# Expert stages of a two-layer diffusion block: the chain up to the first gather reordered, and the query passes of later heads planned further apart

## The reference

```python
def peer(h, w_q, sub_keys, u_tab, v_tab):           # 8 heads, 128 x 128 experts, top 16 per head
    q = (h @ w_q).reshape(b, L, PEER_HEADS, 2, D_HALF)
    scores = jnp.einsum("blhtd,htkd->blhtk", q, sub_keys)
    sv, si = lax.top_k(scores, PEER_TOPK)
    cand_s = sv[..., 0, :, None] + sv[..., 1, None, :]       # 256 candidates
    top_s, pos = lax.top_k(cand_s, PEER_TOPK)
    idx = jnp.take_along_axis(cand_i, pos, axis=-1)
    gate = softmax(top_s)
    act = gelu(jnp.einsum("tkd,td->tk", u_tab[idx], h))
    return jnp.einsum("tk,tkd->td", gate * act, v_tab[idx])

x = layer_norm(alpha * x + gate_row * sublayer((1 + scale) * x + shift))   # shift, scale, gate from c
```

## Time and profile before

| | us |
|---|---|
| median of 3 runs | 5075.4 (5074.77 to 5085.62) |
| profiled execution | 5070.65 |
| its span | 5068.9 |
| PE busy | 3558.4 (70%) |
| DVE busy | 3230.2 (64%) |
| POOL busy | 2215.4 (44%) |
| ACT busy | 1506.1 (30%) |
| first to last gather issued, context | 461.2 to 1210.6 |
| the same, latents of layer 0 | 1676.9 to 3038.9 |
| the same, latents of layer 1 | 3711.5 to 5042.1 |

### The profile page before, as it was taken

The page is one execution under the profiler, slowest core; times in us unless marked ns, Lnnn a source line. Parts: engine busy times, 40 slices in busy tenths (PEclk is TensorE's granted clock), DMA queues, the critical chain, the costliest instruction groups (busy, mean ns, idle before and its releaser), DMA issues. The chain is left out here.

```text
span 5068.9 us, 49208 instructions
## 1 busy us (share of the span) xinstructions
PE 3558.4 (70%) x15992; PEld 1832.1 (36%) x15992; DVE 3230.2 (64%) x6604; ACT 1506.1 (30%) x3708; POOL 2215.4 (44%) x1683
## 2 busy tenths in 40 slices
PE   7887888886678986555555557979888555555555
PEld 5576434332267443111111115877743111111111
DVE  5354687664464567776767766466456777777775
ACT  2342344343151224222222223243222222222221
POOL 3253444442032344555555552334324555555554
PEclk8888999998788998777777778899998777777777
DMA  5435999998602799999999992102268999999998
GB/s 182 171 121 198 390 413 407 415 424 362 231 22 101 274 359 393 416 411 418 403 423 417 411 424 81 67 1 92 84 270 350 415 419 411 417 414 417 420 414 375
DMA packets 251729, 1575.63 MB, mean 311 GB/s; under 512 B 42560, under 2 KB 49216, under 8 KB 65472
## 3 DMA queue, kind: packets, MB, share of 16 engines
q0 software_dynamic: 184320, 1342.26, 64.1%
q1 hardware_dynamic: 67152, 230.23, 12.3%
HBM read 1554.88 MB, written 17.50 MB: 310 GB/s over the span
## 5 line engine op out<-in xcount | busy, mean ns | idle before, releaser
L2337 PE MATMUL banks<-arena 128*64 128x512 f32 x5120 | 1621.0, 771 | 1136.3 <-ACT arena L2169 1135.6
L1953 POOL DMA_INDIRECT arena<-in_experts,arena x1280 | 1499.1, 1171 | 1681.4 <-PE banks L2337 1429.4
L2041 DVE CUSTOM_DVE_ANT_0 arena<-arena,token_copies 128x1024 f32<-128x1024 f32 x1280 | 1640.4, 1298 | 687.5 <-DMA arena<-in_experts,arena 631.5
L2337 PEld LDWEIGHTS banks<-arena 128*64 128x64 f32 x5120 | 391.5, 169 | 2218.4 <-ACT arena L2169 1569.5
L2162 ACT ACTIVATE arena<-arena 128x2 f32<-128x2 f32 x640 | 131.2, 205 | 1830.2 <-DVE arena L2041 1829.2
L281 POOL TENSOR_TENSOR wide_low<-wide_blocks,wide_high 128x1024 fp32r<-128x1024 f32 x136 | 343.5, 2548 | 552.2 <-ACT wide_high L271 552.2
L2169 ACT ACTIVATE arena<-arena 128x64 f32<-128x64 f32 x1280 | 376.0, 340 | 294.1 <-POOL arena L1820 252.7
L2218 PE MATMUL banks<-arena,wide_blocks 128*128 128x512 f32 (+3 forms) x960 | 315.2, 477 | 32.6 <-ACT arena L2071 23.7
L319 PE MATMUL banks<-activation_a,wide_high 128*128 128x512 f32 (+1 forms) x768 | 278.5, 363 | 8.5 <-ACT arena L343 2.7
L2289 PE MATMUL banks<-arena,wide_blocks 128*128 128x512 f32 x576 | 276.6, 618 | 0.0
L321 PE MATMUL banks<-activation_a,wide_low 128*128 128x512 f32 (+1 forms) x768 | 269.4, 351 | 0.0
(11 more groups left out here) (251 smaller groups left out, 4928.2 us busy)
## 6 DMA issues: line engine op xcount, KB each, us to landing
wide_blocks<-in_wide SPq DMA_DIRECT2D x168, 1024.0 KB, 4.8
arena<-in_experts,arena POOLq DMA_INDIRECT x1280, 10.8
pre_scan<-arena SPq DMA_DIRECT2D x16, 256.0 KB, 7.3
arena<-pre_scan SPq DMA_DIRECT2D x16, 256.0 KB, 5.2
residual<-in_tokens SPq DMA_DIRECT2D x6, 512.0 KB, 7.7
arena<-mod_rows SPq DMA_DIRECT2D x6, 512.0 KB, 6.8
norm_rows<-in_keys SPq DMA_DIRECT2D x3, 1024.0 KB, 6.0
pre_z<-arena SPq DMA_DIRECT2D x8, 256.0 KB, 7.4
```

The costliest lines, as they stand in the source:

```text
L1953: pool.indirect_dma_start(out=v.ring[:, g % RING], out_offset=None, in_=io["experts"], in_offset=bass.IndirectOffsetOnAxis(ap=c.idx[:, u % ...
L2041: last = nc.vector.tensor_tensor_reduce(out=u_row, in0=u_row, in1=k.copies[:, n % NJ], scale=1.0, scalar=0.0, op0=ALU.mult, op1=ALU.add, a ...
L2337: mm = nc.tensor.matmul(k.ps[j * QUAD:(j + 1) * QUAD, a + half], v.lhs[:, g % 4, j], v.ring[:, (g * NJ + j) % RING, D + half * BANK:D + (h ...
```

## The change

The stages that end the mixing get a new order of output products and four PSUM banks; the columns are loaded and completed there, into a tensor of their own (`k.nextmod`). In `stage_peer` the first two scores follow the second pass, the later scores stand inside the next pass or behind their own, the first masks stand behind the third gather, and the planned times of the passes are changed: `PROJ` becomes 17.5 for both NT (13 and 17 before), and with NT = 4 the passes from the thirteenth on are planned 16 units apart in place of 8. `stage_finish` is changed as `stage_merge` is.

```diff
-ARENA = A_ROWS + PC_N + HR_N + KT * 32 + 16 + 4 * 288 + 480 - 184
+ARENA = A_ROWS + PC_N + HR_N + KT * 32 + 16 + 4 * 288 + 480 - 200
...
+    k.nextmod = sb("peer_modulation", [P, 2, KT])
...
+def output_order(NT):
+
+    early = [(q, t) for q in range(2) for t in range(NT)]
+    late = [(2, 0), (2, 1), (3, 0)] + [x for t in range(2, NT) for x in ((2, t), (3, t - 1))] + [(3, NT - 1)]
+    return early + late
...
+            sp.dma_start(k.nextmod[:], mods[3 * D:5 * D].rearrange("(a t p) -> p a t", a=2, p=P),
+                         allow_slow_non_contiguous=True).then_inc(k.cols_loaded.sem, 16)
...
-            for n in range(4 * NT):
-                w = take_wide(k, pe, w0 + 14 + n // NT)
-                if n >= 2:
-                    pe.wait_ge(k.mix_read.sem, k.mix_read.at(n - 1))
-                t = n % NT
-
-                product(k, pe, k.ps[:, n % 2, 0:WIDE], lambda kt: mT(kt, slice(t * P, (t + 1) * P)),
+            for n, (quarter, t) in enumerate(output_order(NT)):
+                w = take_wide(k, pe, w0 + 14 + quarter)
+                if n >= 4:
+                    pe.wait_ge(k.mix_read.sem, k.mix_read.at(n - 3))
+
+                product(k, pe, k.ps[:, n % 4, 0:WIDE], lambda kt: mT(kt, slice(t * P, (t + 1) * P)),
                         lambda kt: tuple(part[:, kt] for part in w),
                         ready=(lambda kt: pe.wait_ge(k.merged_lo.sem, k.merged_lo.at(kt + 1))) if n == 0 else None) \
                     .then_inc(k.mix_proj.sem, 1)
...
+            dve.wait_ge(k.cols_loaded.sem, k.cols_loaded.at(16))
+            nc.vector.tensor_scalar(k.nextmod[:, 1], k.nextmod[:, 1], 1.0, None, ALU.add)
...
-            for n in range(4 * NT):
-                t, quarter = n % NT, slice((n // NT) * WIDE, (n // NT + 1) * WIDE)
+            for n, (q, t) in enumerate(output_order(NT)):
+                quarter = slice(q * WIDE, (q + 1) * WIDE)
                 dve.wait_ge(k.mix_proj.sem, k.mix_proj.at(n + 1))
                 dve.drain()
-                nc.vector.tensor_tensor(tmp[:, 0:WIDE], k.ps[:, n % 2, 0:WIDE], g1row[:, quarter], ALU.mult).then_inc(k.mix_read.sem, 1)
+                nc.vector.tensor_tensor(tmp[:, 0:WIDE], k.ps[:, n % 4, 0:WIDE], g1row[:, quarter], ALU.mult).then_inc(k.mix_read.sem, 1)
                 dve.drain()
                 x = k.res[:, tb + t, quarter]
                 nc.vector.scalar_tensor_tensor(x, x, ALPHA, tmp[:, 0:WIDE], ALU.mult, ALU.add)
-                if n >= 3 * NT:
+                if q == 3:
                     layer_norm(k, dve, k.res[:, tb + t], stats, lng, lnb, t)
...
-    REST, STEP = 8.0, 2.0 * NT
-    PROJ = REST + STEP + 1.0
-    proj_at = lambda i: 3.0 + i if i < HEAD else PROJ + sum(2.0 * (x[2] - x[1]) for x in passes[HEAD:i]) + STEP * max(i - N, 0)
-    score_at = lambda i: 4.5 + i - (0.7 if i == HEAD - 1 else 0.0) if i < HEAD else proj_at(i + 2) - 0.1 if i < N - 1 else proj_at(N) + 1.0
-    FIRST = 6.0
+    FIRST, REST, STEP = 6.0, 8.0, 2.0 * NT
+    PROJ = max(REST + STEP, FIRST + 11.0) + 0.5
+    lasts = lambda i: 2.0 * (passes[i][2] - passes[i][1])
+    proj_at = lambda i: 3.0 + i if i < HEAD else PROJ + sum(lasts(j) * (2.0 if j > HEAD + 7 and NT == 4 else 1.0) for j in range(HEAD, i))
+    score_at = lambda i: 4.5 + i // 2 * 2.0 + i % 2 * 0.2 if i < HEAD else proj_at(i) + lasts(i) + 2.0
...
-            sp.dma_start(v.modc, mods[3 * D:5 * D].rearrange("(a t p) -> p a t", a=2, p=P),
-                         allow_slow_non_contiguous=True).then_inc(k.cols_loaded.sem, 16)
...
-                yield FIRST + 14.0
-                c.masks(pool, 0)
...
-                        if n == RING - 1 and u >= 1:
+                        if n == (RING - 1 if u else 2):
                             c.masks(pool, u)
...
-                dve.wait_ge(k.cols_loaded.sem, k.cols_loaded.at(64 if ahead else 16))
-                nc.vector.tensor_scalar(v.modc[:, 1], v.modc[:, 1], 1.0, None, ALU.add).then_inc(k.consts_set.sem, 1)
                 for i, (m, lo, hi) in enumerate(passes):
-                    yield score_at(i) + 0.2 if i < HEAD else proj_at(i + 2) + 1.0
+                    yield score_at(i) + (0.2 if i < HEAD else 1.0 if NT == 2 else 4.0)
...
-                act.wait_ge(k.consts_set.sem, k.consts_set.at(1))
                 for kt in range(KT):
                     act.wait_ge(k.xt_ready.sem, nth(k.xt_ready, kt // 4 + 1))
                     nc.scalar.activation(v.h2T[:, kt, 0:P], k.ps[:, 2 + kt // 4, kt % 4 * P:(kt % 4 + 1) * P], ACT.Identity,
-                                         bias=v.modc[:, 0, kt:kt + 1], scale=v.modc[:, 1, kt:kt + 1]) \
+                                         bias=k.nextmod[:, 0, kt:kt + 1], scale=k.nextmod[:, 1, kt:kt + 1]) \
                         .then_inc(k.h_ready.sem, 1)
...
-                    yield proj_at(i + 1) + 0.5
+                    yield proj_at(i) + lasts(i) + 0.5
                     query(i)
...
+                    between = i > HEAD and score_at(i - 1) < proj_at(i)
+                    if between:
+                        yield score_at(i - 1)
+                        score(i - 1)
                     yield proj_at(i)
...
-                            yield proj_at(i) + STEP / KT * kt
+                            yield proj_at(i) + lasts(i) / KT * kt
+                        if kt == 4 and i > HEAD and not between:
+                            yield score_at(i - 1)
+                            score(i - 1)
...
-                    if 1 <= i < HEAD:
+                    if i < HEAD and i % 2 == 1:
                         yield score_at(i - 1)
                         if i == 1:
                             pe.wait_ge(k.loaded.sem, ld + 16)
                         score(i - 1)
-                    if i == HEAD - 1:
                         yield score_at(i)
                         score(i)
+                    if i == HEAD - 1:
...
-                    if i > HEAD:
-                        yield score_at(i - 1)
-                        score(i - 1)
-                yield proj_at(N) + 1.0
                 finish_used(k, pe)
+                yield score_at(N - 1)
                 score(N - 1)
```

More of the change, by code:

```diff
@@ L1272, in _ @@
                 nc.vector.scalar_tensor_tensor(x, x, ALPHA, tmp[:, 0:WIDE], ALU.mult, ALU.add)
-                if n >= 3 * NT:
+                if q == 3:
                     layer_norm(k, dve, k.res[:, tb + t], stats, lng, lnb, t)
     k.loaded.advance(80)
+    k.cols_loaded.advance(16)
     k.rms_ready.advance(1)
@@ L1572, in _ @@
                     finish_used(k, pe)
[L1573 to L1579, removed]
+            for n, (quarter, t) in enumerate(output_order(NT)):
+                w = take_wide(k, pe, w0 + 4 + quarter)
+                if n >= 4:
+                    pe.wait_ge(k.mix_read.sem, k.mix_read.at(n - 3))
+                product(k, pe, k.ps[:, n % 4, 0:WIDE], lambda kt: mT(kt, slice(t * P, (t + 1) * P)),
                         lambda kt: tuple(part[:, kt] for part in w),
@@ L1668, in peer_views @@
     v = Bag()
-    ring, h2T, scores, lhs, small, spare, modc, pre = carve(k, RING * 2 * D, NT * D, NT * 2048, 8 * QUAD, 2536, D, 16,
+    ring, h2T, scores, lhs, small, spare, pre = carve(k, RING * 2 * D, NT * D, NT * 2048, 8 * QUAD, 2536, D,
                                                             PRE_WORDS[NT])
@@ L1978, in project @@
                 yield PRE
-                dve.wait_ge(k.cols_loaded.sem, k.cols_loaded.at(64))
+                dve.wait_ge(k.cols_loaded.sem, k.cols_loaded.at(48))
                 nc.vector.tensor_scalar(v.modh[:, 1], v.modh[:, 1], 1.0, None, ALU.add).then_inc(k.consts_set.sem, 1)
@@ L2097, in project @@
                 yield PRE + 1.0
-                act.wait_ge(k.consts_set.sem, k.consts_set.at(2))
+                act.wait_ge(k.consts_set.sem, k.consts_set.at(1))
                 for kt in range(KT):
@@ L2263, in project @@
                 pe.wait_ge(k.pre["h"].sem, pre0["h"] + KT)
-                pe.wait_ge(k.cols_loaded.sem, k.cols_loaded.at(64))
+                pe.wait_ge(k.cols_loaded.sem, k.cols_loaded.at(48))
                 for t in range(AN):
@@ L2350, in stage_peer @@
     k.loaded.advance(64)
-    k.cols_loaded.advance(64 if ahead else 16)
-    k.consts_set.advance(2 if ahead else 1)
     if ahead:
+        k.cols_loaded.advance(48)
+        k.consts_set.advance(1)
         for i in range(4):
```

3 lines of the change are left out of this document (1 added, 2 removed).

## The result

The changed kernel takes 5003.4 us (median of 4 runs, 5001.29 to 5009.22) against 5076.9 (4 runs, 5074.77 to 5085.62): ratio 0.9852, 95% interval [0.9836, 0.9867]. Timed again later beside other runs of the kernel before it gave 0.9856 [0.9828, 0.9883]. The forecast was 5018 with a range of 4988 to 5055.

What follows compares the result with a forecast made beforehand. DMA was taken to bound the gather plateaus, TensorE the first part of the latent stages. 11 (context) + (12.3 + 11.1) (first latent) + (6.9 + 16.1) (last) = 57.4 us saved, so 5018 us, range 4988 to 5055.

Steps and rivals of the forecast that it cites:

- The chain: Serial work up to each expert stage's first gather: that gather comes 16.6 (context), 19.1 and 13.7 us (latents) earlier, merges included.
- the columns' term: Columns loaded beforehand, so first activations wait only for transposes: 8.1 us (context), 7.2 (first latent), 1.8 (last) gained.
- The norms' 3.7 us: Norms woven between the last output products: each latent merge 3.7 us shorter, nothing in the context's.
- The masks' 2.3: First masks moved behind three gathers on GpSimd: the first gather starts 2.3 us earlier in each stage.
- the spread's 4.5: Spread issued ahead of the fifth pass: it starts 4.5 us earlier in the latent stages, without delaying the pass.
- Rival B: Earlier starts count in full because DMA, not TensorE, paces the latent stages' first 80 us: 4999 us, chance 0.10.
- The context stage: Passes start 6.6 us and gathers 16.6 us earlier; 11 us counted as gain, near the middle.
- The spacing: Latent stages' later passes at 16 units instead of 8 make DMA the bound: 11.1 and 16.1 us gained.
- the rate sum: TensorE against DMA work per pass distance: 11.4 against 9.0 us in 8 units, 14.4 against 16.7 in 16.
- Rival A: Wider pass distances bring nothing, since TensorE's lag in each pass drains the ring of 8: 5045 us, chance 0.18.
- Rival C: TensorE pauses between the later passes and its clock falls to the 1.2 GHz level: 5200 us, chance 0.05.
- scores at once: Second score right after its copy: 1.4 us in each of three stages; later scores inside the next pass: 0.

Runs made afterwards that it cites:

- second trace of the changed kernel: The changed kernel, unaltered, timed and traced again beside its variants: 5012.1 us, ratio 0.9856 against the kernel before.
- late-spread kernel: Changed kernel with the fifth pass planned at 13 (context) and 17 (latents), so ahead of the first spread as before: 5028.5 us, ratio 0.9899.

## Why the prediction was right, and where it was short

**The chain: right.** 16.6, 15.4 and 10.0 us were worked out up to the first gather within the stages, 17.1, 15.1 and 7.4 were measured. Of the 2.6 us missing in the last stage 1.4 are the columns' term: 0.4 alone in place of 1.8. The norms' 3.7 us came as 4.6 and 3.8. Nothing was paid for the added load and the four banks (no idle time before the adds), so of those bounds the ends at 0 were right.

**What the latent stages make of it: the kind right, the size off.** The prediction let 6.8 us of each be lost to a full TensorE. Up to the 24th gather 4.4 and 4.3 are lost. The masks' 2.3 are lost wholly, as the kernel with masks first shows; of the spread's 4.5 about 0.7 to 3 us remain by the 8th and 16th gather; behind them the late-spread kernel loses more than this, for a reason that stays open. Rival B (all starts in full) falls in the last stage. There, in the trace without spacing, the stage behind its first gather was 6.9 us longer than before, and the 7.3 us won ahead of it within the stage were nearly gone.

**The context stage: too little.** 5.6 us were taken off as a middle, 2.1 were lost.

**The spacing: right in kind, a third too small.** 11.1 and 16.1 us were forecast, 15.3 and 21.7 measured against the kernel without it. Against the second trace of the changed kernel it is 15.9 and 17.3. The term that was mis-sized is the 5 us taken off in each stage for eight uneven passes; no row stood behind it. The gross terms, 16.1 and 21.1, are near what came, but that is in part luck. Both stretches of the earlier trace rows hold 22 gathers; the 26 GB/s between 333 and 307 are two more weight blocks (three in the first, one in the second). The gathers gain the same 16.2 us by the 64th in both stages. Nor is the rate sum confirmed as a rule. It gives the same full DMA at 12 units, where half of the gain is missing. At 16 TensorE has 2.3 us to spare in each cycle. Rival A falls at 16 units; at 12 its kind of loss, each pass a dent in the gathers, is what the time shows. A pass isn't "done in one piece" either: in the timelines groups of products stand between its pieces.

**The first latent stage: a gain that the sum doesn't have.** Behind its first gather this stage gained 20.3 us with 4.3 forecast: 15.3 by the spacing and 5.0 without it. With 4.4 lost at its head, some 9 us came from a place that the prediction didn't look at, the stretch where queries and projection meet. The later place of the projection there was priced at nothing. The kernel that moves it alone gains 5 to 10 us; but the kernel without spacing has the gain too, and its projection isn't moved. A candidate for what gives it there is the new place of the later passes' scores, which was never tried alone. Nor is it settled why queries and projection disturb each other there: TensorE's long waits at that place (5.40 us at one product before) are there with the later projection (6.76 us) and without spacing (4.92 us) too.

**Rival C** (5200) fell: the granted clock was 0.98, then 0.89. The Trainium skill, page "TensorE: Matmul & The Clock Gate", section "HAM oscillation — how this bites in real kernels", tells of a kernel in which each burst starts cold behind its wait. Single places of the last stage agree with it: a group of products that takes 1.94 us took 3.21 behind a wait of 2.85 us, and 3.68 behind the last pass. The other waits between the spaced passes, up to 2.16 us, were followed by groups of 1.94:

```profile
3810.47 3.21 PE L2349 MATMUL banks<-arena 128*64 128x512 f32 x8 [2.85 <-ACT arena L2177]
3839.68 1.94 PE L2349 MATMUL banks<-arena 128*64 128x512 f32 x8 [2.16 <-ACT arena L2177]
3867.09 3.68 PE L2349 MATMUL banks<-arena 128*64 128x512 f32 x8 [4.35 <-ACT arena L2177]
```

So it happens, but far too seldom for C.

**What stays open.** The medians differ by 68 to 74 us, the touched parts of the one pair of traces by 81.5; that pair has a quick start in the kernel before, and a second trace of the changed kernel has 4 us more in its last stage. How much of the difference is scatter of single traces can't be said closer than that. Open are also the 9 us of the first latent stage, the rest of the loss with the spread behind the fifth pass, and both parts of "scores at once", for which no kernel stands alone.

## What to carry to other kernels

Where engines run planned, in-order streams around a ring, price a move by the event that next limits the ring, not by the first event that gets earlier: here the masks' 2 us at the first gather were worth nothing because the ninth waited for a product. A rate sum says where the bound changes, but a plan needs slack beyond it: with none half of the gain was missing, with a seventh of the cycle (2.3 of 16.7 us) all of it was there, and more brought nothing. Read such kernels by several gathers: the 64th alone made 12 units look nearly as good as 16. And when planned times are shifted, look at what changes its order: half a unit (4.5 in one stage) came with a loss of some 20 us, where the later starts themselves are 14.6. Before a side effect is credited with a gain, look whether a kernel without it has the gain too.

## What the runs showed of the hardware that was not expected

The load-bound stretches that no edit touched vary between executions far more than the rest: the first 278.5 to 287.1 us, the reload of states 270.5 to 282.1, while the context's merge stays within 142.5 to 143.8 in all kernels. A small load of columns took 7.2 to 8.8 us to land among a merge's loads (changed kernel, first trace), against 2.7 to 3.2 at the head of an expert stage.
